# One product of ones for each norm, its squares added by VectorE, and the feed-forward layer in one block with its GELU taken chunk by chunk

## What is computed

```
rmsnorm(x, g) = x * rsqrt(mean over the features of x*x + 1e-6) * g

hidden = gelu(conv3(rmsnorm(h, fpre2) @ ffn_w_gate)) * (rmsnorm(h, fpre2) @ ffn_w_up)      # 2816 features
out    = h + rmsnorm(hidden @ ffn_w_down, fpost2)
```

## Time and profile before

| | |
|---|---|
| median of 3 runs | 3315.23 us (3314.86 to 3315.61) |
| the profiled execution | 3316.35 us, of which 3314.4 us from the first to the last instruction |
| PE busy | 3103.0 us (94% of the span) |
| DVE, ACT, POOL busy | 1893.8, 1111.8, 1113.8 us |
| mean granted TensorE clock | 0.967 of full speed |

### The profile page before, as it was taken

One profiled execution on the slowest core, in us unless ns is written; L12 is line 12 of the kernel. 1 busy time (PEld: TensorE's weight loads), 2 busy tenths in 40 slices (PEclk: granted clock), 3 DMA queues, 4 the chain that ended last, 5 costly groups with the idle time before them and its releaser, 6 DMA issues. The chain is left out here.

```text
span 3314.4 us, 38011 instructions
## 1 busy us (share of the span) xinstructions
PE 3103.0 (94%) x14826; PEld 1563.4 (47%) x15096; DVE 1893.8 (57%) x2841; ACT 1111.8 (34%) x1611; POOL 1113.8 (34%) x522
## 2 busy tenths in 40 slices
PE   8899988999798999999999999999998888988997
PEld 4344455445644546464665444444443345433443
DVE  6764996432333858777671355555554853378721
ACT  4334254423332334243433333333333432323221
POOL 1223411333323342434333444444442320224432
PEclk9899999999999999999999999999999987999999
DMA  4212211222122345656567655555552210112321
GB/s 154 96 58 76 102 39 39 89 102 96 70 94 78 134 153 153 197 156 197 153 187 215 229 203 203 203 203 203 204 203 77 96 57 26 58 57 89 108 96 64
DMA packets 265873, 415.84 MB, mean 125 GB/s; under 512 B 148024, under 2 KB 148216, under 8 KB 265312
## 3 DMA queue, kind: packets, MB, share of 16 engines
q1 hardware_dynamic: 265696, 413.40, 37.2%
HBM read 341.56 MB, written 69.22 MB: 124 GB/s over the span
## 5 line engine op out<-in xcount | busy, mean ns | idle before, releaser
L736 POOL TENSOR_TENSOR weights_lo<-weights_as_loaded,weights_hi 128x1024 bf16<-128x1024 f32 x503 | 1112.5, 2214 | 2161.1 <-ACT weights_hi L732 2161.1
L732 ACT ACTIVATE weights_hi<-weights_as_loaded 128x1024 bf16<-128x1024 f32 x507 | 533.2, 1054 | 1263.6 <-PE banks L672 485.6
L2172 DVE TENSOR_TENSOR activation_lo<-activation_f,activation_hi 128x512 bf16<-128x512 f32 x128 | 279.2, 2181 | 312.6 <-ACT activation_hi L2064 312.6
L2033 PE MATMUL banks<-activation_hi,weights_hi 128*128 128x512 bf16 x1004 | 380.6, 379 | 1.1
L2033 PE MATMUL banks<-activation_hi,weights_lo 128*128 128x512 bf16 x1003 | 380.2, 379 | 1.1
L2033 PE MATMUL banks<-activation_lo,weights_hi 128*128 128x512 bf16 x1003 | 380.2, 379 | 1.1
L1985 PE MATMUL banks<-normed_lo,weights_hi 128*128 128x512 bf16 x999 | 378.6, 379 | 1.8
L1985 PE MATMUL banks<-normed_hi,weights_lo 128*128 128x512 bf16 x1000 | 379.0, 379 | 1.3
L1985 PE MATMUL banks<-normed_hi,weights_hi 128*128 128x512 bf16 x991 | 376.3, 380 | 1.2
L2050 ACT ACTIVATE gelu_out<-banks 128x512 f32<-128x512 f32 x128 | 76.2, 596 | 423.4 <-PE banks L1985 416.2
L2155 DVE TENSOR_TENSOR one_hot_b<-iota,pick_column 128x1024 bf16<-128x1024 bf16 x64 | 129.0, 2016 | 144.4 <-PE banks L2006 143.2
(11 more groups left out here) (495 smaller groups left out, 4937.3 us busy)
## 6 DMA issues: line engine op xcount, KB each, us to landing
weights_as_loaded<-in_u_tiles SPq DMA_DIRECT2D x128, 512.0 KB, 3.8
weights_as_loaded<-in_v_tiles SPq DMA_DIRECT2D x128, 512.0 KB, 3.5
gelu_of_dots<-gelu_out SPq DMA_DIRECT2D x128, 256.0 KB, 2.2
activation_f<-gelu_of_dots SPq DMA_DIRECT2D x128, 256.0 KB, 3.8
expert_weight<-expert_weights SPq DMA_DIRECT2D x128, 256.0 KB, 4.0
expert_weights<-weight_grid_even SPq DMA_DIRECT2D x32, 512.0 KB, 4.7
expert_weights<-weight_grid_odd SPq DMA_DIRECT2D x32, 512.0 KB, 5.6
weights_as_loaded<-in_w_xbc SPq DMA_DIRECT2D x24, 512.0 KB, 3.4
```

What stands on the lines that cost most here:

```text
L732: self.nc.scalar.activation(self.whi[:, s, :], self.wraw[:, s, :], ACT.Copy).then_inc(self.w_hi[s], 1)
L736: self.nc.gpsimd.tensor_tensor(self.wlo[:, s, :], self.wraw[:, s, :], self.whi[:, s, :], ALU.subtract).then_inc(self.w_lo[s], 1)
L2033: ins = nc.tensor.matmul(self.ps[:, c, :], v[:, j, c * P:(c + 1) * P], g[:, n % 4, :], start=n + m == 0, stop=n == NV - 1 and m == 2)
L2172: nc.vector.tensor_tensor(glo[:, j, :], gf[:, j, :], ghi[:, j, :], ALU.subtract).then_inc(S["g_lo"], 1)
```

## The change

`Split` and `Sums` no longer multiply each square by ones. ACT's square of chunk 0 goes to one buffer and those of the others to three more in turn; DVE adds each into the first (`add`), and PE multiplies the sum by ones once (`pe`). ACT's wait for a free buffer is now for DVE's addition. The one product of a `Split` comes behind the first output chunk of the next projection (`last_sum`), or behind the four tiles of the outer part of ffn_gate; the one of a `Sums` comes when the last addition is done. In the feed-forward layer, ffn_gate, ffn_up and ffn_down are in one block with what comes before them. GELU is taken per chunk on ACT, two chunks behind the projection; ffn_up's bank is emptied into `few`, from which ACT writes hi and DVE lo, in the place of the hidden chunk; ffn_down waits for these chunk by chunk.

```diff
@@ Split (Sums likewise)
-        self.summed, self.s0 = self.reserve(tag + "_summed", nch)
+        self.added, self.a0 = self.reserve(tag + "_added", nch - 1 if squares is None else 0)
+        self.sums = 1 if squares is None else nch
+        self.summed, self.s0 = self.reserve(tag + "_summed", self.sums)
...
         if c >= 4:
-            act.wait_ge(self.summed, self.s0 + c - 3)
-        self.nc.scalar.activation(self.sq[:, c % 4, 0:self.tok], self.x[:, c, :], ACT.Square).then_inc(self.squared, 1)
+            act.wait_ge(self.added, self.a0 + c - 3)
+        self.nc.scalar.activation(self.square(c), self.x[:, c, :], ACT.Square).then_inc(self.squared, 1)
+
+    def square(self, c):
+        return self.sq[:, 1 + (c - 1) % 3 if c else 0, 0:self.tok]
...
-    def pe(self, pe, c):
-        pe.wait_ge(self.squared, self.q0 + c + 1)
-        self.nc.tensor.matmul(self.k.ps[:, self.bank, 0:self.tok], self.k.ones, self.sq[:, c % 4, 0:self.tok],
-                              start=c == 0, stop=c == self.nch - 1).then_inc(self.summed, 1)
+    def add(self, dve, c):
+        dve.wait_ge(self.squared, self.q0 + c + 1)
+        if c:
+            if c > 1:
+                dve.wait_ge(self.added, self.a0 + c - 1)
+            self.nc.vector.tensor_tensor(self.square(0), self.square(0), self.square(c), ALU.add).then_inc(self.added, 1)
+
+    def pe(self, pe):
+        pe.wait_ge(self.added, self.a0 + self.nch - 1)
+        self.nc.tensor.matmul(self.k.ps[:, self.bank, 0:self.tok], self.k.ones, self.square(0), start=True, stop=True
+                              ).then_inc(self.summed, 1)
@@ beside z
                 split.dve(nc.vector, o - 2)
+                split.add(nc.vector, o - 2)
...
-            if o >= 3:
-                split.pe(nc.tensor, o - 3)
...
-        k.project("ssd", ..., within=late_sums, after={"dve": merge, "act": merge_hi})
+        k.project("ssd", ..., after={"dve": merge, "act": merge_hi, **last_sum(split)})
@@ beside w_out and cross_out
                 split.dve(nc.vector, o - 1)
-        def pe(o, _):
-            if o:
-                split.pe(nc.tensor, o - 1)
+                split.add(nc.vector, o - 1)
                 if other:
-                    other.pe(nc.tensor, o - 1)
+                    other.add(nc.vector, o - 1)
@@ conv3: the last of the three instructions
-            link(nc.vector.scalar_tensor_tensor(y[:, 0:T - 1], r[:, 1:T], w[2], y[:, 0:T - 1], ALU.mult, ALU.add))
+            last = nc.vector.scalar_tensor_tensor(y[:, 0:T - 1], r[:, 1:T], w[2], y[:, 0:T - 1], ALU.mult, ALU.add)
+            if done:
+                last.then_inc(done, 1)
+            else:
+                link(last)
@@ beside w_out2, and between it and ffn_gate
-                         "pe": lambda o, _: own.pe(nc.tensor, o - 1) if o else None})
+                         "dve": lambda o, _: own.add(nc.vector, o - 1) if o else None})
...
                 if c:
                     split.dve(dve, c - 1)
+                    split.add(dve, c - 1)
@@ ffn_gate, ffn_up, ffn_down: one block
+        def gelu(o):
+            nc.scalar.wait_ge(gated, o + 1)
+            nc.scalar.activation(chunk(ff, o), chunk(ff, o), ACT.Gelu_apprx_tanh).then_inc(gelued, 1)
+
+        def gate_act(o, _):
+            if 4 <= o < 12:
+                again.act(nc.scalar, o - 4)
+            if o >= 2:
+                gelu(o - 2)
...
-                  scaled=split.scaled, outer=True, within=sums,
+                  scaled=split.scaled, outer=True,
+                  after={"dve": gate_dve, "act": gate_act,
+                         "pe": lambda o, _: split.pe(nc.tensor) if o == 3 else None})
...
-    with k.together():
-        k.scalar_pass(ff, ff, ACT.Gelu_apprx_tanh)
-        k.project("ffn_up", io["ffn_w_up_2"], FC, 1, k.aT, times(ff), "dve", nxt=io["ffn_w_down_2"],
-                  after=k.then_dve(split_hidden))
-    down = k.sb("ffn_out", [P, DC, T], ctx=s2)
-    with k.together():
+        def hidden(me, o, bank, j):
+            nc.vector.wait_ge(gelued, o + 1)
+            return nc.vector.tensor_tensor(k.few[:, o % 4, :], bank, chunk(ff, o), ALU.mult)
+
+        def hidden_act(o, emptied):
+            nc.scalar.wait_ge(*emptied)
+            nc.scalar.activation(ff2[:, o, 0, :], k.few[:, o % 4, :], ACT.Copy).then_inc(hidden_hi, 1)
+
+        def hidden_rest(o):
+            nc.vector.wait_ge(hidden_hi, o + 1)
+            nc.vector.tensor_tensor(ff2[:, o, 1, :], k.few[:, o % 4, :], ff2[:, o, 0, :], ALU.subtract).then_inc(hidden_lo, 1)
+
+        k.run(act=last_gelus)
+        k.project("ffn_up", io["ffn_w_up_2"], FC, 1, k.aT, hidden, "dve", nxt=io["ffn_w_down_2"],
+                  after={"act": hidden_act, "dve": lambda o, _: hidden_rest(o - 1) if o else None})
...
+        k.project("ffn_down", ..., (ff2[:, :, 0, :], ff2[:, :, 1, :]), copy_to(down), "both", last_k=6,
+                  normed=lambda c: ((hidden_hi, c + 1), (hidden_lo, c + 1)),
                   after={"act": lambda o, emptied: own.act(nc.scalar, o, emptied),
-                         "pe": lambda o, _: own.pe(nc.tensor, o - 1) if o else None})
+                         "dve": lambda o, _: own.add(nc.vector, o - 1) if o else None})
```

More of the change, by code:

```diff
@@ L3080, in dve @@
             split.dve(dve, DC - 1)
+            split.add(dve, DC - 1)
+            if other:
+                other.add(dve, DC - 1)
             split.dve_root(dve)
@@ L3262, in dve @@
         def dve(dve):
+            own.add(dve, DC - 1)
             own.dve_root(dve)
@@ L3270, in dve @@
                     split.dve(dve, c - 1)
+                    split.add(dve, c - 1)
             split.dve(dve, DC - 1)
+            split.add(dve, DC - 1)
             split.dve_root(dve)
[L3274 removed]
+        k.run(act=act, dve=dve, pe=own.pe)
         again = Again(split, k.aT)
[L3277 to L3279 removed]
         def gate_dve(o, emptied):
@@ L3306, in second @@
-    with k.together():
+        gated, gelued = k.sem("hidden_gated"), k.sem("hidden_gelu")
+        def gelu(o):
[6 more added lines that the diff above has]
+                gelu(o - 2)
+        evac, follow = k.conv3(ring, ff, "fconv_w", "fconv_b", FC, k.rs, done=gated)
@@ L3326, in sync @@
                 sp.wait_ge(stored[j], 16)
-        k.run(sync=sync, act=own.act_root, dve=dve, pe=lambda pe: own.pe(pe, DC - 1))
+        k.run(sync=sync, act=own.act_root, dve=dve, pe=own.pe)
     s2.close()
```

83 lines of the change are left out of this document (46 added, 37 removed).

## The result

The changed kernel takes **3262.1 us** (3261.6 to 3262.8, 4 runs) where the kernel before takes 3315.1 us beside it (3313.5 to 3315.6): a ratio of 0.984, 95% interval 0.982 to 0.986, so 53 us less. The forecast was 3259.1 us with a range of 3250 to 3274. The profiled execution has a span of 3261.0 us.

A forecast was written before the change was run, and what follows sets the result against it. PE was taken to bound the kernel, busy 94% of the span. Terms of 12.9 + 7.5 + 6.0 + 3.6 + 6.0 + 4.8 + 7.9 + 1.0 + 6.4 = 56.1 us gave 3259.1 us, range 3250 to 3274.

The forecast's parts named there:

- Wherever a large product runs, a microsecond taken from PE is a microsecond of the kernel: Whole kernel: PE, busy 94% of the span, is the bound unless another engine has less slack, as in ffn_gate.
- w_out's tail: End of w_out: PE waits 1.5 us for VectorE on the last chunk, leaving a gain of 7.5 us (5 to 9.0).
- Without them PE waits for the next weights ... 2.8 us gained: w_out2's outer part: three products by ones removed, PE waits for POOL's weights, 2.8 us gained, not 4.7.
- The loss at the root: End of w_out2: the last addition waits for POOL's subtraction, so the root starts 1.8 us later; 0.3 if free.
- ffn_gate's outer part: In front of ffn_gate: seven products by ones fewer at 0.86 us each, 6.0 us gained.
- What of it reaches PE is between nothing and all: In ffn_gate: VectorE saves at most 2.9 us by not waiting for the convolution's last step; 1.0 us taken as gain.
- 2.8 us, the gate's backlog on VectorE: First boundary, ffn_gate to ffn_up: PE waits only 2.8 us for the bank; 7.9 us gained (6.5 to 9.2).
- I take the middle: First boundary: a clock fall in the short pause costs nothing or 2.7 us; 1.3 us was subtracted.
- The second boundary and the end: ffn_up to ffn_down gains 6.4 us with no new wait; ffn_down with its last norm gains 4.8 us.
- VectorE as the bound beside z: Rival beside z and w_out: additions meeting POOL make rounds 6.5 us, not 5.18; 3278 us, chance 0.08.
- GELUs holding up the roundings: Rival at the first boundary: ScalarE's GELUs delay rounding or VectorE's backlog grows; 3268 to 3281 us, chance 0.14.
- The clock did not fall for lack of pauses: Rival behind ffn_gate: PE's work without pause lowers the clock to 1.2 GHz; all gain lost or 3374 us, chance 0.03.

The follow-up runs named there:

- norms_only: The kernel before with only the additions of Split and Sums, the feed-forward layer staying in three blocks: 3276.3 us.
- filled: The changed kernel plus idle PE products, 8 behind w_out2's outer part and 20 behind ffn_gate's last tile: 3258.9 us.
- lone_last: The changed kernel with the last square in Sums not added by VectorE but multiplied by ones separately on PE: 3257.2 us.
- two_repairs: The changed kernel with GELU four chunks behind the projection and each last square left out of the additions: 3255.2 us.
- gelu_later: The changed kernel with each GELU of ffn_gate four chunks behind the projection instead of two: 3258.5 us.
- next_bank: The changed kernel with ffn_up's ring of four banks beginning at bank 2 instead of bank 0: 3255.3 us.

## Why the prediction was right, and where it was off

**The bound.** "Wherever a large product runs, a microsecond taken from PE is a microsecond of the kernel": right for z, w_out, cross_out and all that follows the first boundary, 37.9 of the 53.4 us, each within 0.3 us of its term. The price of 0.86 us for a product by ones fits all of them, and VectorE had room (it waits 0.68 us a round beside z). norms_only confirms it as a whole: 39.2 us, where the forecast's terms for the norms sum to 40.8 and w_out2 alone missed by 2.3.

**What was luck.** 2.0 of the 53.4 us come from the two stretches in which nothing was changed (1.3 and 0.7), and the start of z alone differs by 3.8 us between the kernels. Without them the gain is 51.4 us against 56.1, and the time would be some 3264 us: still in the range, but 5 us off and not 3. The misses below nearly all go one way, toward less gain than forecast.

**w_out's tail** was 1.5 us in the forecast and is 0.56 + 0.79 = 1.35.

**w_out2: 1.3 us, not 3.6.** The step that failed is "Without them PE waits for the next weights ... 2.8 us gained". The start came 2.6 us earlier, but the pause of 1.98 us that replaced the three products lowered the clock, and eight slow steps took 1.7 back. The products by ones had kept PE at work (waits of 0.2 to 0.8 us between them before); filled shows the 1.7 us directly. I had weighed the clock at the first boundary and not here. The loss at the root is 2.1 us (1.8 forecast, 2.10 = 3.66 - 1.56 us from the square's end to the root): the mechanism, POOL's hold on the addition, was right, and lone_last shows its price of 1.9 us.

**ffn_gate's outer part: 5.4, not 6.0.** There were ten slow steps before and thirteen now: 3 x 0.21 us. Their number is not bound to the pause in front of them: behind the same 7.9 us it is seven in filled and nine in lone_last and two_repairs, and the outer part takes 28.6 us in all three. What sets the number stays open.

**In ffn_gate and at the first boundary: 6.8, not 8.9.** "What of it reaches PE is between nothing and all": all of 2.4 us reached PE's end of ffn_gate, and none of it the start of ffn_up, since that start hangs on VectorE. From the scale to the emptying of chunk 20 VectorE took 99.85 us before (2943.55 to 3043.40) and 99.80 after. The saved wait of 22 x 0.13 us was lost to the locked rounds: gelu_later, which unties them, needs 96.95. So the failed step is the pause of "2.8 us, the gate's backlog on VectorE" (its own figures give 3044.09 - 3041.37 = 2.72): the emptying that it names was the right one, but the sum let PE gain 1.0 us in ffn_gate and VectorE as much. PE gained 2.4 and VectorE nothing, so the pause is 2.7 + 2.4 = 5.1 us, as the trace has it from the end of the last turn (3003.51 to 3008.62; the profile's 4.95 counts from the end of the record). The second miss is the clock, "I take the middle" of 0 and 2.7 us: thirteen steps took 5.33 us where 2.81 are due, so it cost 2.5. Both are one cause, a pause, and the bank was the cause of the pause: with the other bank the 5.1 + 2.5 us are there, 7.64 measured.

**The second boundary and the end**: 11.1, not 11.2. The cover held: ffn_down never waited for a hidden chunk.

**The range.** "All low ends together give 3269, all high ends 3254" doesn't follow from the ranges given. The low ends of w_out, w_out2, the first boundary and ffn_gate take 2.5 + 0.6 + 1.4 + 1.0 us away, which gives 3264.6, and the high ends add 1.5 + 1.5 + 1.3 + 1.9, which gives 3252.9. The result lies in either.

**Rivals.** VectorE as the bound beside z did not happen (idle 0.68 us a round). GELUs holding up the roundings did happen in a weak form: they shaped the rounds, for some 2.7 us of pause, not the 8.9 and more of that rival. The clock did not fall for lack of pauses: from 3014 to 3240 the granted clock is 1.00, and in next_bank, where PE has not even the pause at the boundary, it is 1.00 from 3001.45 to 3231.

## What to carry to other kernels

A product that is taken out of a stretch in which PE waits next for something else gives back only the difference to that wait, and if a pause takes its place the clock must be priced too: here a pause of 2 us cost 1.7 us more. Where two stages are joined, ask which bank (or slot) the second one begins with: here a recently used bank waited for nearly the whole backlog of the engine that empties it, and one used two chunks earlier for none of it. And before tuning an engine that is full, look whether anyone waits for it: the locked rounds looked costly and cost nothing once the bank was changed.

## What the runs showed of the hardware that I had not expected

- The granted clock fell behind a pause of 1.98 us (eight slow steps at once), fell late behind 2.26 us (five fast steps, then eight slow), and did not fall behind 2.52 us in lone_last (1.00 from 3005.97 to 3009.00). Behind 7.9 us in front of ffn_gate seven, nine or thirteen slow steps stood, by the kernel. The pause's length alone doesn't say it.
- POOL, ScalarE and VectorE can hold each other in step: a 0.75 us operation took 2.50 us in six rounds running, each exactly 4.50 us.
- A product of ones takes 0.86 us of PE when it stands among others, but its end comes later when PE was idle in front of it: its records span 1.28 us after 3.95 us of pause (2.08 in filled, at a granted clock of 0.50), 1.13 after 2.18, 1.02 without.
- An edit of a few instructions' order on VectorE beside cross_out made cross-attention, cross_out and the experts together 2.0 us longer (1609.3 to 1607.3 us) in all three kernels that had it: 0.5 is a wait of PE behind cross_out, and 1.4 a clock that came back later behind an unchanged pause of 9.3 us.
